# Latent attention in a two-block transformer kernel: queries and keys without position made channels first

## The chip, the cores and the metric

The kernel is one program on 1 core of one Trainium2 chip. The metric is device time in microseconds (us) of one launch, lower is better. Before the change it was timed in three runs: 1926.68 us in the median, from 1926.54 to 1927.67. TensorE does the matrix products, VectorE and ScalarE the elementwise work, GpSimd a few small steps, and SyncE issues the weight loads. The engines run their own instruction streams in order and wait for each other with semaphores.

## The reference

The first block runs twice (two layers), the second once. The change touches the latent attention (MLA) of the first block:

```python
def first_block(x, norm_g, w_in, diff_lambda, ..., mla_q_norm_g, w_uq, mla_kv_norm_g, w_ukv, w_out, final_norm_g):
    for l in range(DEPTH):                                   # DEPTH = 2, seq = 256, D_MODEL = 2048
        h = _rms_norm(x, norm_g[l])
        proj = jnp.einsum('bsd,de->bse', h, w_in[l])
        q_a, k_a, v_a, z_a, c_q, c_kv, k_r, z_b = jnp.split(proj, split_points, axis=-1)
        o_a = _diff_attention(qa, ka, va, lam, rel_bias_table)        # 8 heads, two softmaxes each
        o_a = _rms_norm(o_a, diff_subln_g[l]) * (1.0 - lambda_init)
        o_a = o_a.reshape(b, seq, DIFF_WIDTH) * jax.nn.silu(z_a)

        q_b = jnp.einsum('bsr,re->bse', _rms_norm(c_q, mla_q_norm_g[l]), w_uq[l])      # 512 -> 8 x (128 + 64)
        q_b = q_b.reshape(b, seq, MLA_HEADS, MLA_NOPE_DIM + MLA_ROPE_DIM)
        q_nope, q_rope = q_b[..., :MLA_NOPE_DIM], q_b[..., MLA_NOPE_DIM:]
        q_rope = _apply_rope(q_rope, cos[:, None, :], sin[:, None, :])
        kv = jnp.einsum('bsr,re->bse', _rms_norm(c_kv, mla_kv_norm_g[l]), w_ukv[l])    # 512 -> 8 x (128 + 128)
        kv = kv.reshape(b, seq, MLA_HEADS, MLA_NOPE_DIM + MLA_V_DIM)
        k_nope, v_b = kv[..., :MLA_NOPE_DIM], kv[..., MLA_NOPE_DIM:]
        k_rope = _apply_rope(k_r, cos, sin)
        o_b = _mla_attention(q_nope, q_rope, k_nope, k_rope, v_b)     # softmax((qn.kn + qr.kr) * scale, causal) v
        o_b = o_b.reshape(b, seq, MLA_WIDTH) * jax.nn.silu(z_b)

        x = x + jnp.einsum('bse,ed->bsd', jnp.concatenate([o_a, o_b], axis=-1), w_out[l])
    return _rms_norm(x, final_norm_g)
```

The second block (convolution, pooling, cross attention, a gated feed-forward) is not touched.

## The kernel before

**Products in three passes.** All inputs are 32-bit floats. A weight is loaded in units of 128 x 1024 numbers (512 KB) into one of four slots of `stage`. ScalarE rounds a unit to `w_hi` (L395), VectorE makes the rest `w_lo = stage - w_hi` (L400, `rest_unit`), and TensorE multiplies hi by hi, hi by lo and lo by hi into PSUM. Activations are kept channels first, split the same way (`xT`, `mT`). The slot of a unit is free once TensorE has used it (`unit_used`), so ScalarE and VectorE prepare unit u+3 (`LEAD`) while TensorE multiplies unit u.

**Two shapes of a unit.** `product_rows` (L437 to L439) holds the activations in the array and streams 512 weight columns: 12 matmuls of 512 columns in a unit, and the result has tokens on the partitions. `product_cols` (L453, L460) holds the weights and streams the tokens, hi and lo side by side: 8 matmuls of 512 columns (weight hi by both halves) and 8 of 256 (weight lo by hi); the result has channels on the partitions, in two halves that are added afterwards. The first block uses rows nearly everywhere, the feed-forward uses columns.

**PSUM.** `acc` is two pairs of banks, used in turn by the chunks of a stage. A product that starts a chunk waits until the pair has been read out (`banks_free`, counted by `acc_free0` and `acc_free1`). `aux` holds one bank for transposes (`tb`), two for scores, one for weights and outputs of heads.

**The stages of a layer.** After the first 56 units of w_in come the latent stage (32 units, here u = 0 to 31), the gate stage (32 units of w_in for the gates) and w_out (32 units). In the latent stage, units 0 to 15 make c_q and c_kv (512 columns each), 16 and 17 the rope key, 18 to 23 w_uq (three chunks of 512 columns, two units each), 24 to 31 w_ukv (four chunks). Heads of the differential attention are strewn in between, one in four units: after unit 4h the weights of head h-1 are transposed (L1117) and queries and keys of head h (L517), after unit 4h+1 come the outputs of head h-1 (L1123 to L1125) and the scores of head h (L1136). VectorE then makes the maxima (`diff_max`, L1995 to L2002) and two units later the weights (`diff_weights`, L2008 to L2014). The latents are turned to channels first after units 10, 11, 18 and 19 (`C_TURN`: transposes by TensorE, scale L528, round L535, rest L540). Their inverse roots `rstd_c` are made by `rsqrt` (L559 to L564, eleven small steps that wait for each other) at u = 19, after ScalarE's squares (L1707, at u = 16); ScalarE multiplies them in when it copies the w_uq and w_ukv chunks out of PSUM (L1720).

**The MLA heads** stand in the gate stage, one in four units. After unit 4h+2 `turn` (L517) transposes two blocks of queries (`qb`) and two of keys (`kvb`) of head h without position, ScalarE copies them to `qkT` (L1592), and after the next unit `mla_scores` (L1153, L1154) multiplies them. GpSimd applies the rope to `qb` and `kz` during the latent stage (L1002 to L1021).

The order of the work on each engine is written out by hand, by unit numbers.

## Time and profile before

| | us |
|---|---|
| median of three runs | 1926.68 |
| the profiled execution's own time | 1927.88 |
| its span, first to last instruction | 1926.1 |
| TensorE busy | 1914.7 (99%) |
| VectorE busy | 1433.1 (74%) |
| ScalarE busy | 1081.9 (56%) |
| GpSimd busy | 46.2 (2%) |
| mean granted TensorE clock | 0.998 of full speed |

The latent stage of layer 0 lies at about 179 to 286 us of the span, that of layer 1 at about 621 to 728; the gate stages follow. Busy time of an engine says how much it did, not whether anyone waited for it. For TensorE the starts of consecutive matmuls tell what one costs: a matmul's duration in the profile (0.39 us) is longer than the distance to the next one (0.23 us), since they overlap.

### The profile page before, as it was taken

The page shows a single profiled execution, that of the slowest core. Times are in us where ns is not written, and L with a number is a line of the kernel's source. Part 1 is how long each engine was busy: PE and PEld are TensorE (multiplying, and loading weights), DVE is VectorE, ACT ScalarE, POOL GpSimd, SP SyncE. Part 2 cuts the span into 40 slices and gives each one's busy share as a digit, 9 for nine tenths or more (in the row PEclk, how much of TensorE's full clock was granted, in tenths as well). Part 3 has the DMA queues.
Part 4 walks back from the last instruction along what each step waited for, and adds up shares of the span by engine and source line. Part 5 has one row for each costly group of instructions (what it writes and reads, how often), then busy time and mean ns, then how long its engine had stood idle before and what let it go on. Part 6 is the DMA issues. An engine that isn't in the chain of part 4 may idle for free.

```text
span 1926.1 us, 26620 instructions
## 1 busy us (share of the span) xinstructions
PE 1914.7 (99%) x9721; PEld 1623.2 (84%) x9721; DVE 1433.1 (74%) x2059; ACT 1081.9 (56%) x1598; POOL 46.2 (2%) x74
## 2 busy tenths in 40 slices
PE   9999999999999999999999999999999999999997
PEld 7888888888888888888888888888888888888886
DVE  7777675556877675655767766888878878899898
ACT  6555676655545676654644444655555555555554
POOL 1000030000000030000100000000000000000000
PEclk9999999999999999999999999999999999999999
DMA  9964445565665455555666455665666666666654
GB/s 347 309 210 133 143 154 158 151 206 185 209 209 167 139 162 176 142 164 186 212 187 194 154 166 184 186 185 182 199 188 191 188 185 191 190 219 197 204 192 161
DMA packets 248059, 361.29 MB, mean 188 GB/s; under 512 B 15505, under 2 KB 134497, under 8 KB 247457
## 3 DMA queue, kind: packets, MB, share of 16 engines
q1 hardware_dynamic: 246112, 353.15, 58.5%
q0 software_dynamic: 1568, 6.60, 1.0%
q8 instruction: 57, 0.93, 0.2%
q10 hardware_dynamic: 288, 0.33, 0.0%
q14 instruction: 34, 0.27, 0.0%
HBM read 356.88 MB, written 3.16 MB: 187 GB/s over the span
## 4 chain that ended last, share of the span: by engine, by line
PE 98%; DVE 1%; DMA 0%; ACT 0%; issue 0%; SPq 0%; DVEq 0%; ACTq 0%
PE acc L460 22%; PE acc L453 12%; PE acc L437 11%; PE acc L439 11%; PE acc L438 11%; PE acc L1206 4%; PE acc L1207 4%; PE acc L1205 4%; PE acc L1468 3%; PE acc L1469 3%; PE acc L1467 3%; PE aux L517 2%; PE aux L1468 1%; PE aux L1467 1%; PE aux L1469 1%; PE aux L1136 1%
## 5 line engine op out<-in xcount | busy, mean ns | idle before, releaser
L400 DVE TENSOR_TENSOR sb_w_lo<-sb_stage,sb_w_hi 128x1024 fp32r<-128x1024 f32 x476 | 583.0, 1227 | 272.2 <-ACT sb_w_hi L395 265.7
L395 ACT ACTIVATE sb_w_hi<-sb_stage 128x1024 fp32r<-128x1024 f32 x476 | 502.2, 1057 | 348.8 <-PE acc L453 122.7
L460 PE MATMUL acc<-sb_xT,sb_w_hi 128*128 128x512 f32 x1856 | 445.7, 391 | 0.0
L460 PEld LDWEIGHTS acc<-sb_xT,sb_w_hi 128*128 128x128 f32 x1856 | 340.8, 188 | 65.8
L453 PEld LDWEIGHTS acc<-sb_xT,sb_w_lo 128*128 128x128 f32 x1856 | 238.7, 191 | 9.3
L453 PE MATMUL acc<-sb_xT,sb_w_lo 128*128 128x256 f32 x1856 | 243.0, 283 | 0.0
L437 PE MATMUL acc<-sb_w_hi,sb_mT 128*128 128x512 f32 x544 | 217.3, 399 | 0.0
L439 PE MATMUL acc<-sb_w_hi,sb_mT 128*128 128x512 f32 x544 | 212.2, 390 | 0.0
L438 PE MATMUL acc<-sb_w_lo,sb_mT 128*128 128x512 f32 x544 | 212.1, 390 | 0.0
L437 PE MATMUL acc<-sb_w_hi,sb_xT 128*128 128x512 f32 x384 | 155.9, 406 | 0.0
L439 PE MATMUL acc<-sb_w_hi,sb_xT 128*128 128x512 f32 x384 | 150.0, 391 | 0.0
L438 PE MATMUL acc<-sb_w_lo,sb_xT 128*128 128x512 f32 x384 | 149.9, 390 | 0.0
L437 PEld LDWEIGHTS acc<-sb_w_hi,sb_mT 128*128 128x128 f32 x544 | 102.2, 188 | 22.7 <-issue 1.0
L439 PEld LDWEIGHTS acc<-sb_w_hi,sb_mT 128*128 128x128 f32 x544 | 102.1, 188 | 22.0
L438 PEld LDWEIGHTS acc<-sb_w_lo,sb_mT 128*128 128x128 f32 x544 | 102.3, 188 | 19.7
L1205 PE MATMUL acc<-sb_w_hi,sb_xT 128*128 128x512 f32 x220 | 85.7, 389 | 0.0
L1207 PE MATMUL acc<-sb_w_hi,sb_xT 128*128 128x512 f32 x220 | 85.6, 389 | 0.0
L1206 PE MATMUL acc<-sb_w_lo,sb_xT 128*128 128x512 f32 x220 | 85.6, 389 | 0.0
L439 PEld LDWEIGHTS acc<-sb_w_hi,sb_xT 128*128 128x128 f32 x384 | 72.1, 188 | 15.7
L437 PEld LDWEIGHTS acc<-sb_w_hi,sb_xT 128*128 128x128 f32 x384 | 72.2, 188 | 13.9
L740 ACT ACTIVATE sb_w_hi<-sb_pair_stage 128x1024 fp32r<-128x1024 f32 (+1 forms) x50 | 48.2, 982 | 62.2 <-DVE sb_pair_stage L753 53.5
L438 PEld LDWEIGHTS acc<-sb_w_lo,sb_xT 128*128 128x128 f32 x384 | 72.3, 188 | 12.7
(437 smaller groups left out, 2871.1 us busy)
## 6 DMA issues: line engine op xcount, KB each, us to landing
sb_stage<-w_in SPq DMA_DIRECT2D x232, 512.0 KB, 4.3
sb_stage<-w_up SPq DMA_DIRECT2D x176, 512.0 KB, 3.7
sb_stage<-w_out SPq DMA_DIRECT2D x96, 512.0 KB, 4.3
sb_stage<-w_down SPq DMA_DIRECT2D x54, 512.0 KB, 6.7
...
```

The source lines that it names most:

```text
L395: act.activation(w_hi[:, j % RING, 0:size], stage[:, j % RING, 0:size], ACT.Copy).then_inc(hi_ready, 1)
L400: dve.tensor_tensor(w_lo[:, j % RING, 0:size], stage[:, j % RING, 0:size], w_hi[:, j % RING, 0:size].bitcast(F32), ALU.subtract).then_inc( ...
L437: pe.matmul(o, x_hi, hi[:, k, :], start=first and k == 0, stop=False)
L438: pe.matmul(o, x_hi, lo[:, k, :], start=False, stop=False)
L439: mm = pe.matmul(o, x_lo, hi[:, k, :], start=False, stop=last and k == nk - 1)
L453: mm = pe.matmul(acc[:, 2 * pair + c, 0:SEQ], lo[:, k, c * P:(c + 1) * P], xT[:, k0 + k, 0, :], start=False, stop=False)
L460: mm = pe.matmul(acc[:, 2 * pair + c, :], hi[:, k, c * P:(c + 1) * P], both, start=first and k == 0, stop=last and k == 3)
L1205: pe.matmul(o, a(0), hi, start=start, stop=False)
L1206: pe.matmul(o, a(0), lo, start=False, stop=False)
L1207: return pe.matmul(o, a(1), hi, start=False, stop=stop)
L1467: pe.matmul(o, a(0), hi, start=start, stop=False)
L1468: pe.matmul(o, a(0), lo, start=False, stop=False)
```

## The change

- The weights w_uq and w_ukv are reordered on the host: all parts without position first, then the rope parts of w_uq and the values of w_ukv.
- In the latent stage, units 18 to 21 now make the queries without position, 24 to 27 the keys, in the shape by columns: four channel tiles of weights in a unit for 256 output channels (two heads), so each of these units is a chunk of its own. `product_latent_cols` issues 8 matmuls of 512 columns, then 8 of 256. Units 22 and 23 (rope parts, one chunk) and 28 to 31 (values, two chunks) stay by rows.
- Such a chunk is read out in two steps: ScalarE copies the right half to `cols_half` (`copy_cols`), VectorE adds the left half to it (`add_cols`) and frees the pair. Both stand one unit later in their streams, ahead of the preparation of a weight unit. The rows chunks are copied by ScalarE without a factor (`copy_rows`).
- Queries and keys are then channels first already: the eight transposes-of-four of the MLA heads in each layer and ScalarE's eight copies go.
- Roots: ScalarE scales c_kv itself before its turn (two instructions at u = 18), and VectorE applies the queries' root when it scales the scores (`query_scale`); `rsqrt` of the latents stands at u = 16 instead of 19. The turns of c_kv stand after units 19 and 21 instead of 18 and 19. `diff_max(4)` stands at u = 17 ahead of the rest of a unit, where it stood behind it.
- The mask is two blocks wide, and VectorE makes the scaled scores of a head in two steps of 256 and 128 columns where it took steps of 128 and 256.

```diff
-DIFF_TB = [2, 3, 4, 7, 8, 11, 12, 13]
-C_TURN = {10: (0, 0, 5), 11: (0, 1, 6), 18: (1, 0, 9), 19: (1, 1, 10)}
+DIFF_TB = [2, 3, 4, 7, 8, 10, 12, 13]
+C_TURN = {10: (0, 0, 5), 11: (0, 1, 6), 19: (1, 0, 9), 21: (1, 1, 11)}
...
+QUERY_COLS, KEY_COLS = {18 + n: n for n in range(4)}, {24 + n: n for n in range(4)}
+C_QUERY, C_ROPE, C_KEY, C_VALUE, C_Z, C_OUT = 9, 13, 14, 18, 20, 24
...
+        def product_latent_cols(pe, base, j, k0, pair):
+
+
+            pe.wait_ge(lo_ready, base + (j + 1))
+            hi, lo = (w[:, j % RING, :].rearrange("p (k n) -> p k n", n=256) for w in (w_hi, w_lo))
+            tiles = [(k, c) for k in range(4) for c in range(2)]
+            for k, c in tiles:
+                pe.matmul(acc[:, 2 * pair + c, :], hi[:, k, c * P:(c + 1) * P],
+                          mT[:, k0 + k, :, :].rearrange("p h t -> p (h t)"), start=k == 0, stop=False)
+            for k, c in tiles:
+                mm = pe.matmul(acc[:, 2 * pair + c, 0:SEQ], lo[:, k, c * P:(c + 1) * P], mT[:, k0 + k, 0, :],
+                               start=False, stop=k == 3)
+            mm.then_inc(unit_used, 1)
...
+        query_pair = lambda n: qb[:, n % 2, n // 2 * 512:(n // 2 + 1) * 512].rearrange("p (h t) -> p h t", h=2)
+        key_pair = lambda n: kvb[:, 0, n * 512:(n + 1) * 512].rearrange("p (h t) -> p h t", h=2)
+        query_of, key_of = (lambda h: query_pair(h // 2)[:, h % 2, :]), (lambda h: key_pair(h // 2)[:, h % 2, :])
+        value_of = lambda h, t: kvb[:, 1, t * WIDTH + h * DV:t * WIDTH + (h + 1) * DV]
+        output_of = lambda h, t: kvb[:, 0, h * SEQ + t * DV:h * SEQ + (t + 1) * DV]
+        rope_rows = lambda t: qb[:, t, WIDTH:WIDTH + HEADS * ROPE]
...
-                            pe.matmul(o, qkT[:, q * P:(q + 1) * P], qkT[:, 2 * P:2 * P + keys], start=True, stop=False)
+                            pe.matmul(o, query_of(h)[:, q * P:(q + 1) * P], key_of(h)[:, 0:keys], start=True, stop=False)
...
+                            if u in QUERY_COLS:
+                                c, i = C_QUERY - 6 + QUERY_COLS[u], 0
+                            if u in KEY_COLS:
+                                c, i = C_KEY - 6 + KEY_COLS[u], 0
+                            if u >= 28:
+                                c, i = C_VALUE - 6 + (u - 28) // 2, u % 2
...
+                        elif u in QUERY_COLS or u in KEY_COLS:
+                            product_latent_cols(pe, base, U_QKV + u, 0 if u < 24 else 4, c % 2)
...
+                            if j == 1:
+                                pe.wait_ge(ckv_scaled, layer + 1)
...
+                    def copy_cols(u, chunk):
+
+                        multiplied(act, quads * 4, U_QKV + u)
+                        if chunk not in (C_QUERY, C_KEY):
+                            evacuated(act, pairs, chunk - 1)
+                        pair = chunk % 2
+                        act.activation(cols_half[:, :, :], acc[:, 2 * pair:2 * pair + 2, SEQ:2 * SEQ], ACT.Copy)\
+                           .then_inc(cols_copied, 1)
+
+                    def copy_rows(u, chunk, dst):
+
+                        multiplied(act, quads * 4, U_QKV + u)
+                        for t in range(T):
+                            ins = act.activation(dst(t), acc[:, 2 * (chunk % 2) + t, :], ACT.Copy)
+                        ins.then_inc(acc_free[chunk % 2], 1)
+
+                    value_rows = lambda c: lambda t: kvb[:, 1, t * WIDTH + c * 512:t * WIDTH + (c + 1) * 512]
+
                     for u in range(32):
+                        if u - 1 in QUERY_COLS:
+                            copy_cols(u - 1, C_QUERY + QUERY_COLS[u - 1])
+                        if u - 1 in KEY_COLS:
+                            copy_cols(u - 1, C_KEY + KEY_COLS[u - 1])
+                        if u == 24:
+                            copy_rows(23, C_ROPE, rope_rows)
+                        if u == 30:
+                            copy_rows(29, C_VALUE, value_rows(0))
                         rounded(U_QKV + u)
+                        if u == 18:
+                            act.wait_ge(c_rstd, layer + 1)
+                            for t in range(T):
+                                ckv = qb[:, t, RANK:2 * RANK]
+                                ins = act.activation(ckv, ckv, ACT.Copy, scale=rstd_c[:, T + t:T + t + 1])
+                            ins.then_inc(ckv_scaled, 1)
...
-                        if u == 20 or (u > 20 and u % 2 == 1):
-                            c = (u - 19) // 2
-                            act.wait_ge(c_rstd, layer + 1)
-                            multiplied(act, quads * 4, U_QKV + 19 + 2 * c)
-                            for t in range(T):
-                                r = (0 if c < 3 else T) + t
-                                dst = qb[:, t, c * 512:(c + 1) * 512] if c < 3 else \
-                                    kvb[:, t, (c - 3) * 512:(c - 2) * 512]
-                                ins = act.activation(dst, acc[:, 2 * ((9 + c) % 2) + t, :], ACT.Copy,
-                                                     scale=rstd_c[:, r:r + 1])
-                            ins.then_inc(acc_free[(9 + c) % 2], 1)
                     for u in range(32):
+                        if u == 0:
+                            copy_rows(31, C_VALUE + 1, value_rows(1))
...
+                    def add_cols(chunk, dst):
+
+                        dve.wait_ge(cols_copied, layer * 8 + (chunk - C_QUERY if chunk < C_ROPE else chunk - C_KEY + 4) + 1)
+                        pair = chunk % 2
+                        dve.tensor_tensor(dst, acc[:, 2 * pair:2 * pair + 2, 0:SEQ], cols_half[:, :, :], ALU.add)\
+                           .then_inc(acc_free[pair], 1)
+
                     add_rows_qkv(5)
                     dve.wait_ge(bias_back, 16)
                     for u in range(32):
-                        if u == 18:
+                        if u - 1 in QUERY_COLS:
+                            add_cols(C_QUERY + QUERY_COLS[u - 1], query_pair(QUERY_COLS[u - 1]))
+                        if u - 1 in KEY_COLS:
+                            add_cols(C_KEY + KEY_COLS[u - 1], key_pair(KEY_COLS[u - 1]))
+                        if u == 16:
+                            step(dve.tensor_tensor(key_fold, ident[:, 0:ROPE], ident[:, ROPE:P], ALU.add))
+                            dve.wait_ge(c_squared, layer * 4 + 4)
+                            rsqrt(step, dve, rstd_c[:, :], sumsq_c[:, :], 4, RANK, done=c_rstd)
+                        if u == 17:
                             multiplied(dve, base, U_QKV + 17)
                             step(dve.tensor_copy(key_sum, acc[:, 0, SEQ:2 * SEQ]))
                             dve.tensor_tensor(key_sum, acc[:, 0, 0:SEQ], key_sum, ALU.add).then_inc(acc_free[0], 1)
-                        if u == 16:
-                            step(dve.tensor_tensor(key_fold, ident[:, 0:ROPE], ident[:, ROPE:P], ALU.add))
+                            diff_max(4)
                         if u % 4 == 3:
                             diff_weights(u // 4)
-                        if u == 19:
+                        if u in (19, 21):
                             j, t, use = C_TURN[u]
                             turn_scale(dve, tb0 + use, gain0 + (2 + 2 * j + t), gain_c[:, 4 * j:4 * j + 4])
                         rest(U_QKV + u)
@@ -2131,14 +2194,14 @@
                             evacuate_scaled(dve, base, U_QKV + u, j, 512, lambda t: qb[:, t, j * RANK:(j + 1) * RANK], rstd)
                         if u in C_TURN:
                             j, t, use = C_TURN[u]
-                            if u != 19:
+                            if j == 0:
                                 turn_scale(dve, tb0 + use, gain0 + (2 + 2 * j + t), gain_c[:, 4 * j:4 * j + 4])
                             turn_rest(dve, turn0 + (2 + 2 * j + t), token_part(mT, j, t, 0), token_part(mT, j, t, 1))
-                        if u % 4 == 1:
+                        if u == 20:
+                            dve.wait_ge(c_rstd, layer + 1)
+                            step(dve.tensor_scalar(query_scale[:, :], rstd_c[:, 0:T], MLA_SCALE, None, ALU.mult))
+                        if u % 4 == 1 and u != 17:
                             diff_max(u // 4)
-                        if u == 19:
-                            dve.wait_ge(c_squared, layer * 4 + 4)
-                            rsqrt(step, dve, rstd_c[:, :], sumsq_c[:, :], 4, RANK, done=c_rstd)
```

How the streams move, at three places. First VectorE in the latent stage of layer 0, from the fold of the rope key on; the names are `acc` (PSUM pair of a chunk), `sb_w_lo` (rest of a weight unit), `sb_turn_f` and `sb_mT` (turn of a latent), `sb_newton_v` (the root). Before:

```order
L2120 TENSOR_TENSOR sb_qb<-acc,sb_qb 128x256
L400 TENSOR_TENSOR sb_w_lo<-sb_stage,sb_w_hi 128x1024
L528 TENSOR_TENSOR sb_turn_f<-aux,sb_gain_c 128x512
L540 TENSOR_TENSOR sb_mT<-sb_turn_f,sb_mT 128x4x128
L2008 RECIPROCAL sb_inv_sum<-sb_row_sum 128x4
L2010 SCALAR_TENSOR_TENSOR sb_mix_f<-sb_row_sum,sb_lam_l,sb_inv_sum 128x2
L2012 SCALAR_TENSOR_TENSOR sb_s<-sb_s,sb_mix_f 128x256
L2014 SCALAR_TENSOR_TENSOR sb_s<-sb_s,sb_mix_f 128x128
L528 TENSOR_TENSOR sb_turn_f<-aux,sb_gain_c 128x512
L400 TENSOR_TENSOR sb_w_lo<-sb_stage,sb_w_hi 128x1024
L540 TENSOR_TENSOR sb_mT<-sb_turn_f,sb_mT 128x4x128
L559 TENSOR_SCALAR sb_newton_v<-sb_sumsq_c 128x4
```

And after the change, from the last step of the root to the first sum of halves:

```order
L580 SCALAR_TENSOR_TENSOR sb_rstd_c<-sb_newton_t,sb_rstd_c 128x4
L402 TENSOR_TENSOR sb_w_lo<-sb_stage,sb_w_hi 128x1024
L2183 COPY sb_qb<-acc 128x256
L2184 TENSOR_TENSOR sb_qb<-acc,sb_qb 128x256
L2043 SCALAR_TENSOR_TENSOR sb_s<-aux,sb_bias 128x512
L2045 SCALAR_TENSOR_TENSOR sb_s<-aux,sb_bias 128x256
L2048 TENSOR_REDUCE sb_neg_max<-sb_s 128x2
L2049 TENSOR_REDUCE sb_neg_max<-sb_s 128x2
L2050 TENSOR_SCALAR sb_neg_max<-sb_neg_max 128x4
L402 TENSOR_TENSOR sb_w_lo<-sb_stage,sb_w_hi 128x1024 x2
L2167 TENSOR_TENSOR sb_qb<-acc,sb_cols_half 128x512
```

The root has moved from behind the turns to ahead of the rest of unit 19; the fold of the rope key (L2183, L2184), the maxima of head 4 (L2043 to L2050) and two rests stand between it and the first sum of halves (L2167), which frees a pair.

Second, VectorE between the first two sums of halves, after the change:

```order
L2167 TENSOR_TENSOR sb_qb<-acc,sb_cols_half 128x512
L2056 RECIPROCAL sb_inv_sum<-sb_row_sum 128x4
L2058 SCALAR_TENSOR_TENSOR sb_mix_f<-sb_row_sum,sb_lam_l,sb_inv_sum 128x2
L2060 SCALAR_TENSOR_TENSOR sb_s<-sb_s,sb_mix_f 128x256
L2062 SCALAR_TENSOR_TENSOR sb_s<-sb_s,sb_mix_f 128x128
L544 TENSOR_TENSOR sb_turn_f<-aux,sb_gain_c 128x512
L402 TENSOR_TENSOR sb_w_lo<-sb_stage,sb_w_hi 128x1024
L556 TENSOR_TENSOR sb_mT<-sb_turn_f,sb_mT 128x4x128
```

The weights of head 4, a turn's two steps and a rest stand in front of the sum of unit 19's halves, which is the next row.

Third, TensorE around units 19 to 21 of the latent stage. Before, the end of unit 18, the turn behind it and the begin of unit 19:

```order
L439 MATMUL acc<-sb_w_hi,sb_mT 128x512
L517 MATMUL aux<-sb_ident,sb_qb 128x128 x4
L437 MATMUL acc<-sb_w_hi,sb_mT 128x512
L438 MATMUL acc<-sb_w_lo,sb_mT 128x512
L439 MATMUL acc<-sb_w_hi,sb_mT 128x512
```

After, the turn behind unit 19, unit 20, and the transposes behind it:

```order
L533 MATMUL aux<-sb_ident,sb_qb 128x128 x4
L481 MATMUL acc<-sb_mT,sb_w_hi 128x512 x8
L484 MATMUL acc<-sb_mT,sb_w_lo 128x256 x8
L1142 MATMUL aux<-sb_ident,sb_s 128x128 x3
L533 MATMUL aux<-sb_ident,sb_qa 128x128 x2
L533 MATMUL aux<-sb_ident,sb_kz 128x128 x2
```

Unit 20 (L481, L484) begins a chunk on the pair that unit 18 used; before, units 20 and 21 shared a chunk on the other pair than 18 and 19.

## Rows read from the trace of the kernel before

**Rows 1.** Page, part 1: busy us (share of the span) xinstructions.

```profile
PE 1914.7 (99%) x9721; PEld 1623.2 (84%) x9721; DVE 1433.1 (74%) x2059; ACT 1081.9 (56%) x1598; POOL 46.2 (2%) x74
```

**Rows 2.** Waits of TensorE: line, who released it, us in total, times, longest.

```profile
PE acc L1526 <- DVE sb_w_lo L747: 0.9, 1, 0.9
```

**Rows 3.** Timeline, TensorE, gate stage: start us, us, engine line operation.

```profile
296.57 0.38 PE L517 MATMUL aux<-sb_ident,sb_qb 128*128 128x128 f32 x2
...
296.92 0.48 PE L437 MATMUL acc<-sb_w_hi,sb_xT 128*128 128x512 f32 x1
297.24 0.40 PE L438 MATMUL acc<-sb_w_lo,sb_xT 128*128 128x512 f32 x1
...
309.59 0.38 PE L517 MATMUL aux<-sb_ident,sb_qb 128*128 128x128 f32 x2
...
309.95 0.47 PE L437 MATMUL acc<-sb_w_hi,sb_xT 128*128 128x512 f32 x1
```

**Rows 4.** The chain that ended last, in the second block: start us, us.

```profile
944.07 3.65 PE acc L460 x16
947.73 1.91 PE acc L453 x16
```

**Rows 5.** Timeline, TensorE: an undisturbed unit by rows and what follows it.

```profile
286.23 0.39 PE L437 MATMUL acc<-sb_w_hi,sb_xT 128*128 128x512 f32 x1
...
288.95 0.49 PE L1117 MATMUL aux<-sb_ident,sb_s 128*128 128x128 f32 x3
```

**Rows 6.** Timeline, TensorE: starts of unit 18 and the turn behind it, layer 0.

```profile
238.98 0.50 PE L437 MATMUL acc<-sb_w_hi,sb_mT 128*128 128x512 f32 x1
...
241.83 0.60 PE L517 MATMUL aux<-sb_ident,sb_qb 128*128 128x128 f32 x4
```

**Rows 7.** Timeline, ScalarE: end of the last square of the latents, layer 0.

```profile
237.49 0.19 ACT L1707 ACTIVATION_READ_ACCUMULATOR sb_junk<-sb_qb 128x1 f32 x1
```

**Rows 8.** Timeline, VectorE, latent stage of layer 0.

```profile
239.94 0.68 DVE L1995 SCALAR_TENSOR_TENSOR sb_s<-aux,sb_bias 128x512 f32<-128x512 f32 x1
...
242.12 0.42 DVE L2119 COPY sb_qb<-acc 128x256 f32<-128x256 f32 x1
...
242.91 1.22 DVE L400 TENSOR_TENSOR sb_w_lo<-sb_stage,sb_w_hi 128x1024 fp32r<-128x1024 f32 x1
...
246.03 0.17 DVE L2008 RECIPROCAL sb_inv_sum<-sb_row_sum 128x4 f32<-128x4 f32 x1
...
247.16 0.68 DVE L528 TENSOR_TENSOR sb_turn_f<-aux,sb_gain_c 128x512 f32<-128x512 f32 x1
247.75 1.22 DVE L400 TENSOR_TENSOR sb_w_lo<-sb_stage,sb_w_hi 128x1024 fp32r<-128x1024 f32 x1
248.89 0.69 DVE L540 TENSOR_TENSOR sb_mT<-sb_turn_f,sb_mT 128x512 fp32r<-128x512 f32 x1
249.49 0.17 DVE L559 TENSOR_SCALAR sb_newton_v<-sb_sumsq_c 128x4 f32<-128x4 f32 x1
...
251.54 1.22 DVE L400 TENSOR_TENSOR sb_w_lo<-sb_stage,sb_w_hi 128x1024 fp32r<-128x1024 f32 x1
```

**Rows 9.** Timeline, last products: VectorE's rest, and TensorE's start behind it.

```profile
1908.69 1.22 DVE L747 TENSOR_TENSOR sb_w_lo<-sb_stage,sb_w_hi 128x1024 fp32r<-128x1024 f32 x1
...
1909.97 0.50 PE L1526 MATMUL acc<-sb_w_hi,sb_act_T 128*128 128x512 f32 x1 [0.95 <-DVE sb_w_lo L747]
```

**Rows 10.** Timeline, TensorE: first matmul behind the scores of head 7.

```profile
280.66 0.50 PE L437 MATMUL acc<-sb_w_hi,sb_mT 128*128 128x512 f32 x1
```

**Rows 11.** Timeline, VectorE: maxima of that head, idle before them in brackets.

```profile
280.78 0.69 DVE L1995 SCALAR_TENSOR_TENSOR sb_s<-aux,sb_bias 128x512 f32<-128x512 f32 x1 [1.49 <-PE aux L1136]
```

**Rows 12.** Timeline, VectorE: two rests beside GpSimd's rope, then maxima.

```profile
262.71 3.48 DVE L400 TENSOR_TENSOR sb_w_lo<-sb_stage,sb_w_hi 128x1024 fp32r<-128x1024 f32 x2 [0.42 <-ACT sb_w_hi L395]
267.35 0.69 DVE L1995 SCALAR_TENSOR_TENSOR sb_s<-aux,sb_bias 128x512 f32<-128x512 f32 x1 [1.16 <-PE aux L1136]
```

**Rows 13.** Timeline, GpSimd: a step of the rope of the queries.

```profile
263.51 1.60 POOL L1018 TENSOR_TENSOR sb_kz<-sb_qb,sb_rope 128x256 f32<-128x256 f32 x1
```

120 lines of the change are left out of this document (59 added, 61 removed).

## The prediction

> **What bounds the kernel now.** I read part 1 of the page first: TensorE is busy 99% of the span, VectorE 74% [rows 1]. The waits of TensorE come next. Behind the first microseconds they name one that counts, 0.9 us in the last products [rows 2]; in both latent stages and both gate stages it waits for nobody. So TensorE's stream is the critical path, and the change is worth what it takes out of that stream, less what it puts in, less every wait that it creates there: nothing downstream gives a wait back. The third view is the timeline, for two questions: what an instruction costs on TensorE (the distance between starts, not the duration shown), and at what time VectorE gets to each step of the latent stage of layer 0. Layer 1 runs the same streams, so each result counts twice.
>
> **What goes.** Eight turns of the MLA heads in each layer, four transposes each. Alone, a turn starts at 296.57, the next product at 296.92, and the matmul behind that 0.32 us later instead of 0.23: 0.35 + 0.09 = 0.44 us. Seven of the eight stand right behind the transposes of another head's weights, where the slow first matmul is paid anyway: 309.59 to 309.95, 0.36 us [rows 3]. A layer: 0.44 + 7 x 0.36 = 2.96; both: **-5.9 us**. ScalarE's copies to qkT go with them; ScalarE is 56% busy and nobody on the path waits for it there, so they are worth nothing directly.
>
> **What TensorE gets.** Sixteen units change shape, eight in a layer. By columns, 16 long matmuls start within 3.65 us and 16 short ones within 1.91 [rows 4], so a unit is half of the sum, 2.78 us. By rows an undisturbed unit takes 286.23 to 288.95, 2.72 us [rows 5]. 0.06 x 16 = **+1.0 us**. The scores read queries and keys from other tiles in the same shape: 0, since the matmul is the same.
>
> **What waits.** A chunk was two units; a chunk by columns is one. TensorE begins unit 20 on the pair that unit 18 filled, 2.8 us after unit 18's end plus a turn, and in that time ScalarE must copy one half and VectorE must add the other. The question is when VectorE gets there. I follow its new order with the old durations.
>
> The root now stands ahead of the rest for unit 19 and waits for ScalarE's squares, which end at 237.68 [rows 7]. From there: the root, 249.49 to 251.54, 2.05 us; a rest, 247.75 to 248.89, 1.14; fold of the rope key, 242.12 to 242.91, 0.79; maxima of head 4, 239.94 to 242.12, 2.18; two more rests, 2.28 [rows 8]. That is 246.12. The sum of halves reads 512 columns from PSUM and from SBUF. No row shows it; the nearest is the first step of the maxima, 0.68 with the same kinds of input [rows 8]; from below the two small steps of the fold bound it at 0.4, from above a rest at 1.22. I take 0.68: 246.80, and 0.06 until TensorE starts, as at 1909.91 to 1909.97 [rows 9]: 246.86. TensorE gets there at 238.98 + 2.85 (unit 18 starts and ends as before [rows 6]) + 0.06 (its new shape) + 2.78 (unit 19) + 0.36 (the turn behind it) = 245.03. **Wait at unit 20: 1.83 us.** The copy on ScalarE is not the last to come, since ScalarE can take it as soon as unit 18 ends at 241.9. The rest for unit 20 itself is ready at 245.0, a tie.
>
> Unit 21 needs the pair of unit 19. VectorE, from 246.12: the sum 0.60 in its stream, weights of head 4 1.13 (246.03 to 247.16), scale 0.59, rest 1.14, rest of the turn 0.60 (248.89 to 249.49), sum 0.68 [rows 8]: 250.86, with the start 250.92. TensorE: 246.86 + 2.78 + 0.09 + seven transposes of 0.09 = 250.36. **Wait: 0.56 us.**
>
> Units 22 to 26 I find covered: behind unit 21 TensorE has the fold of the key, outputs, scores and a turn, over 2 us, and unit 22 and 23 are one chunk. Unit 27 waits for the sum of unit 25's halves, and that stands behind the maxima of head 6, whose scores TensorE issues only behind unit 25. VectorE begins such maxima 0.12 us after the next product begins [rows 10, 11]; 0.12 + 2.18 + 0.68 + 0.06 = 3.04 against 2.87 for unit 26. **Wait: 0.17 us,** and a first matmul of 0.50 instead of 0.39 behind a wait [rows 9], 0.28 together. At units 20 and 21 that slow first matmul is already paid for the transposes ahead of them.
>
> While TensorE waits, its queue holds the products of the unit and the heads' steps behind it; ScalarE and VectorE lose nothing, they are ahead. A layer: 1.83 + 0.56 + 0.28 = 2.67; both: **+5.3 us**.
>
> **GpSimd's neighbourhood.** Its rope of the queries overlaps the rests for units 27 and 28: the two took 3.48 us, where two rests alone take 2.4, beside a step of GpSimd's that took 1.60 [rows 12, 13]. Maxima in the same stretch kept their 0.69 [rows 12]. By my reading, steps with two SBUF inputs collide, steps that read PSUM do not. Before, the lead of three units covered it. Now, between units 24 and 28, each pair waits for a sum behind a rest, so up to the 1.1 us lost there could appear at unit 27 or 28: from 0 to 1.1 in a layer. The layer's rope starts at about the same unit, but falls on other steps; I take 0.25 in a layer, nearer to nothing, since only one rest stands between the scores of head 6 and the sum that matters: **+0.5 us**. The Trainium skill (GPSIMD Engine Reference, Specifications) says that GpSimd shares its SBUF interfaces with VectorE and contends with instructions that have two SBUF inputs; the trace agrees, with 3.48 for two rests and 0.69 for the maxima. By it, the new sums themselves, which have one SBUF input, would stay at 0.68 beside the rope, and only rests and weights would stretch.
>
> **Edits at nothing.** The two scalings of c_kv by ScalarE are new, and the turn behind unit 19 waits for them. They can begin when the root is there, at 239.7, and are due when unit 19 ends, at 244.7: 5 us for 1024 columns, which VectorE takes 1.22 for in a rest [rows 8]. With that cover gone they would cost what they are late. Maxima of MLA heads: 256 and 128 columns instead of 128 and 256, the same. Loads: the same number and size at the same places of SyncE's queue, in rows half as long; three units of lead cover them. GpSimd waits for one chunk instead of two and must be done eight units later.
>
> **The sum.** -5.9 + 1.0 + 5.3 + 0.5 = **+0.9 us**. The profiled execution took 1927.88, so 1928.8 by its own time; it stands 1.2 above the median of the runs, 1926.68, and against that median I predict **1927.6 us**. A measurement of this kernel can tell about 0.2%, 3.9 us, from no change.
>
> **The rivals.**
> - *Exchange of transposes for waits*, as above. For it: the chain to unit 20 has no slack left in it and is made of measured steps. Against: it assumes that no step of VectorE starts earlier than in my order. Its own range, with 0.3 us of error on each of three waits and 0 to 1.1 for the collision: 1925.5 to 1930.5. Chance 0.66.
> - *The waits are hidden*: the pairs come free in time, because TensorE reaches unit 20 later than I think or the squares end earlier. For it: before, TensorE never waited here, and VectorE has a quarter of its time free [rows 1]. Against: it would need 1.8 us, all of it at one place. -5.9 + 1.0 = -4.9: 1921.8. Chance 0.11.
> - *Slower, by GpSimd's collision at unit 27*: the rope of the queries falls on the rests of units 28 and 29, and the sums of units 25 and 26 slip by 1.1 us each, one after the other, with no lead to take it. It decides if a collision stands between the scores of head 6 and unit 28. 2.2 us a layer in place of 0.25: +0.9 + 3.9 = +4.8, 1931.5. For it: 3.48 for two rests [rows 12]. Against: GpSimd's steps that collide are few. Chance 0.16.
> - *The change doesn't do what it says*: the root comes one unit sooner, but nothing that waits for it was late, and being sooner is what puts 2.05 us and a wait for the squares ahead of three rests. If the rests for units 19 and 20 come late as well by about 0.5 us each, that is +2 over the sum: 1929.6. Chance 0.07.
>
> **How the numbers follow.** Faster by over 0.2%: only the second case, 0.11. Slower: the third, and a tail of the first and last, 0.17. Within: 0.72. The range is to leave out 2 in 10: it reaches from 1923.5, between the first and the second case, to 1931.5, the price of the third.
>
> **What would show it.** Right: MATMULs of `turn` on `sb_kvb` in the gate stage halved, and those on `sb_qb` down to the latents' own; waits of TensorE in the latent stage released by VectorE's L2167, two of 1.8 and two of 0.6 us, at about 245 and 250 of the span and 442 us later; the gate stage shorter by 3 us, the latent stage longer by about 3. Wrong: no wait at L481 (then 1921.8), or waits over 1 us at units 26 to 28 with long L402 beside GpSimd (then 1931).

## The result, and the profile of the changed kernel

| | before | changed |
|---|---|---|
| median of 13 runs each, us | 1927.27 | 1931.46 |
| their range | 1926.54 to 1928.48 | 1929.73 to 1933.09 |
| ratio, 95% interval | | 1.0021 [1.0014, 1.0028] |
| span of the profiled execution | 1926.1 | 1930.0 |
| its own time | 1927.88 | 1931.84 |

The change made the kernel 4.2 us slower, 0.21%, and the interval of the ratio does not reach down to 1. I had forecast 0.9 us more, 1927.6, with a range to 1931.5. The number lies inside the range, but at its very end, and the loss is over four times the forecast one: that it is inside is luck.

The page of the changed kernel, part 1 and the first line of part 4, against [rows 1]:

```profile
PE 1912.6 (99%) x9721; PEld 1621.2 (84%) x9721; DVE 1443.8 (75%) x2077; ACT 1073.2 (56%) x1586; POOL 48.7 (3%) x74
...
PE 94%; DVE 4%; DMA 1%; ACT 1%; issue 0%; SPq 0%; DVEq 0%; ACTq 0%
```

TensorE's busy time fell by 2.1 us, and the span still grew by 3.9: TensorE stands still for 6 us that it did not stand still before. In the chain, VectorE's share went up from 1% to 4%. The waits of TensorE say where (line <- who released it: us in total, times, longest), against [rows 2]:

```profile
PE acc L481 <- DVE sb_qb L2167: 4.0, 4, 1.8
PE acc L481 <- DVE sb_kvb L2167: 1.6, 2, 0.8
PE acc L1555 <- DVE sb_w_lo L771: 1.4, 1, 1.4
```

L481 is the first matmul of a unit by columns, L2167 VectorE's sum of halves, which frees the pair. Four waits are at units 20 and 21, two at unit 27. The timeline of TensorE in layer 0, at these places (start, us, and the idle time before in brackets):

```profile
239.50 2.14 PE L481 MATMUL acc<-sb_mT,sb_w_hi 128*128 128x512 f32 x8
...
242.44 2.12 PE L481 MATMUL acc<-sb_mT,sb_w_hi 128*128 128x512 f32 x8
...
245.35 0.60 PE L533 MATMUL aux<-sb_ident,sb_qb 128*128 128x128 f32 x4
247.72 2.11 PE L481 MATMUL acc<-sb_mT,sb_w_hi 128*128 128x512 f32 x8 [1.77 <-DVE sb_qb L2167]
...
251.78 0.50 PE L481 MATMUL acc<-sb_mT,sb_w_hi 128*128 128x512 f32 x1 [0.24 <-DVE sb_qb L2167]
...
274.89 0.50 PE L481 MATMUL acc<-sb_mT,sb_w_hi 128*128 128x512 f32 x1 [0.80 <-DVE sb_kvb L2167]
```

The idle time in brackets is not the whole loss. Without a wait, the next matmul starts 0.16 to 0.25 us ahead of the shown end of the one before. Counted from that follow-on, unit 20 loses 2.02 us, unit 21 0.49, unit 27 0.96, and unit 24, which the view of waits does not list at all, 0.24.

To say where time went I cut each layer at three starts on TensorE that both kernels have: the first product of the rope key (L477, now L493), the transposes of the rope key in the first gate unit (`ident,sb_kz`), and the first product of the output weights on `mT` (L437, now L439). Below, "latent stage" means the first stretch: the second half of the latent stage, from u = 16 on, and the first gate unit. The rest of the gate stage is the second stretch. Here are the three starts of layer 0 before the change, then of the changed kernel:

```profile
232.93 0.39 PE L477 MATMUL acc<-sb_xT,sb_w_hi 128*128 128x512 f32 x1
...
289.27 0.38 PE L517 MATMUL aux<-sb_ident,sb_kz 128*128 128x128 f32 x2
...
399.61 0.48 PE L437 MATMUL acc<-sb_w_hi,sb_mT 128*128 128x512 f32 x1
```

```profile
233.46 0.39 PE L493 MATMUL acc<-sb_xT,sb_w_hi 128*128 128x512 f32 x1
...
294.33 0.27 PE L533 MATMUL aux<-sb_ident,sb_kz 128*128 128x128 f32 x1
...
401.43 0.48 PE L439 MATMUL acc<-sb_w_hi,sb_mT 128*128 128x512 f32 x1
```

| us | before | changed | difference |
|---|---|---|---|
| latent stage, layer 0 (layer 1) | 56.34 (56.35) | 60.87 (60.87) | +4.53 (+4.52) |
| gate stage | 110.34 (110.34) | 107.10 (107.10) | -3.24 (-3.24) |
| both stages, both layers | | | +2.57 |
| from the first gate stage's end to layer 1's start | | | +0.27 |
| ahead of layer 0's latent stage | | | +0.53 |
| from layer 1's gate stage to the last wait | | | +0.02 |
| the last wait (L1555) and behind it | | | +0.5 |

The stages repeat to 0.05 us from layer to layer and, below, between kernels that do the same there; the two ends of the program do not. The product that stands at 9.51 us before and at 9.84 after starts anywhere from 8.67 to 9.84 in all the profiles, and the last wait takes from nothing to 1.6.

Of the 0.53 us ahead of layer 0's latent stage, 0.33 are there at that product. The other 0.2 grow bit by bit between 196 and 233 us, in units 0 to 15, and 0.2 of the 0.27 between the layers grow in the same units of layer 1. That part repeats: from about 16 us to the rope key it is 217.4 us before and 217.6 in eight of the ten kernels below that keep the change. What makes it, no run shows. So 3.0 us of the change's loss are located; the other 0.9 of this pair of profiles lie where single executions differ. The measured ratio allows 2.7 to 5.4 us.

The gate stage is where the turns were. Before, weights and a turn behind them took 0.68 us, from this start to the product at 309.95 [rows 3]; now it is 0.25 (before, then the changed kernel):

```profile
309.27 0.38 PE L1117 MATMUL aux<-sb_ident,sb_s 128*128 128x128 f32 x2
```

```profile
313.83 0.49 PE L1142 MATMUL aux<-sb_ident,sb_s 128*128 128x128 f32 x3
314.08 0.48 PE L439 MATMUL acc<-sb_w_hi,sb_xT 128*128 128x512 f32 x1
```

### The profile page after: what moved, and what is told of

It reads as the page before. It is cut to its first block, busy times and chain, and to the rows that moved or that the text cites. A ratio compares the mean times of both kernels' runs of the same rounds, so it can differ in the third digit from the quotient of the medians.

```text
span 1930.0 us, 26624 instructions
## 1 busy us (share of the span) xinstructions
PE 1912.6 (99%) x9721; PEld 1621.2 (84%) x9721; DVE 1443.8 (75%) x2077; ACT 1073.2 (56%) x1586; POOL 48.7 (3%) x74
## 4 chain that ended last, share of the span: by engine, by line
PE 94%; DVE 4%; DMA 1%; ACT 1%; issue 0%; SPq 0%; DVEq 0%; ACTq 0%
PE acc L462 22%; PE acc L455 11%; PE acc L439 10%; PE acc L440 10%; PE acc L441 10%; PE acc L1225 4%; PE acc L1227 4%; PE acc L1226 4%; PE acc L1496 2%; PE acc L1497 2%; PE acc L1498 2%; PE aux L533 1%; PE acc L481 1%; PE aux L1496 1%; PE aux L1497 1%; PE aux L1161 1%
## 5 line engine op out<-in xcount | busy, mean ns | idle before, releaser
L439 PE MATMUL acc<-sb_w_hi,sb_mT 128*128 128x512 f32 x480 | 191.4, 399 | 0.0
L440 PE MATMUL acc<-sb_w_lo,sb_mT 128*128 128x512 f32 x480 | 187.3, 390 | 0.0
L441 PE MATMUL acc<-sb_w_hi,sb_mT 128*128 128x512 f32 x480 | 187.2, 390 | 0.0
L439 PE MATMUL acc<-sb_w_hi,sb_xT 128*128 128x512 f32 x384 | 156.4, 407 | 0.0
L439 PEld LDWEIGHTS acc<-sb_w_hi,sb_mT 128*128 128x128 f32 x480 | 90.2, 188 | 19.8 <-issue 1.0
L441 PEld LDWEIGHTS acc<-sb_w_hi,sb_mT 128*128 128x128 f32 x480 | 90.2, 188 | 19.5
L440 PEld LDWEIGHTS acc<-sb_w_lo,sb_mT 128*128 128x128 f32 x480 | 90.3, 188 | 17.5
L439 PEld LDWEIGHTS acc<-sb_w_hi,sb_xT 128*128 128x128 f32 x384 | 72.2, 188 | 14.2
```

The source lines that it names most:

```text
L439: pe.matmul(o, x_hi, hi[:, k, :], start=first and k == 0, stop=False)
L440: pe.matmul(o, x_hi, lo[:, k, :], start=False, stop=False)
L441: mm = pe.matmul(o, x_lo, hi[:, k, :], start=False, stop=last and k == nk - 1)
```

## Who holds unit 20

VectorE and then ScalarE of the changed kernel, layer 0, ahead of unit 20:

```profile
238.31 0.17 DVE L575 TENSOR_SCALAR sb_newton_v<-sb_sumsq_c 128x4 f32<-128x4 f32 x1 [2.33 <-ACT sb_junk L1764]
...
240.38 1.22 DVE L402 TENSOR_TENSOR sb_w_lo<-sb_stage,sb_w_hi 128x1024 fp32r<-128x1024 f32 x1
...
244.40 0.17 DVE L2050 TENSOR_SCALAR sb_neg_max<-sb_neg_max 128x4 f32<-128x4 f32 x1
244.48 2.35 DVE L402 TENSOR_TENSOR sb_w_lo<-sb_stage,sb_w_hi 128x1024 fp32r<-128x1024 f32 x2
246.98 0.69 DVE L2167 TENSOR_TENSOR sb_qb<-acc,sb_cols_half 128x512 f32<-128x512 f32 x1
```

```profile
244.60 0.51 ACT L1627 ACTIVATE sb_s<-sb_s,sb_neg_max 128x256 f32<-128x256 f32 x1 [1.65 <-DVE sb_neg_max L2050]
...
246.38 0.57 ACT L1721 ACTIVATE sb_cols_half<-acc 128x512 f32<-128x512 f32 x1
```

The sum (L2167) takes 0.69 us, as forecast. It starts at 246.98 because two things end there nearly together: two rests on VectorE, at 246.83, and ScalarE's copy of the other half, at 246.95. Unit 18 was done at 242.4, but the copy stands in ScalarE's queue behind the exponentials of head 4, which wait for VectorE's maxima. The prediction followed VectorE alone and said that the copy was "not the last to come". The copy is the last to come, by a little: VectorE starts a step up to 0.1 us ahead of the shown end of the one before (the rests at 244.48, with the negation shown to 244.57), so behind the rests alone the sum could have started at about 246.75. It starts 0.23 later, 0.03 behind the copy's end.

## The experiments

All ran in five rounds beside the kernel before on the same chip (the changed kernel's row is that of the result): 5 runs of e2, 6 of e7, 10 or 11 of each of the others. The ratios are to the kernel before, whose median was 1926.96 to 1927.06 in these rounds; the last two columns are the two stretches of layer 0.

| kernel | median us | ratio, 95% interval | latent | gate |
|---|---|---|---|---|
| changed | 1931.46 | 1.0021 [1.0014, 1.0028] | 60.87 | 107.10 |
| e1 copies | 1930.10 | 1.0016 [1.0007, 1.0025] | 60.61 | 107.10 |
| e2 sums | 1934.35 | 1.0042 [1.0029, 1.0056] | 63.13 | 107.10 |
| e3 both | 1927.36 | 1.0002 [0.9993, 1.0011] | 59.27 | 107.10 |
| e4 root | 1928.01 | 1.0005 [0.9996, 1.0014] | 59.65 | 107.09 |
| e5 ordered | 1924.83 | 0.9988 [0.9979, 0.9997] | 58.04 | 107.10 |
| e6 GpSimd short | 1929.78 | 1.0014 [1.0005, 1.0023] | 60.05 | 107.10 |
| e7 no turns (of before) | 1920.94 | 0.9966 [0.9954, 0.9979] | 56.37 | 107.03 |
| e8 root alone (of before) | 1931.63 | 1.0025 [1.0015, 1.0034] | 58.42 | 110.36 |
| e9 last | 1922.67 | 0.9979 [0.9970, 0.9988] | 57.23 | 107.10 |
| e10 no negation | 1928.30 | 1.0005 [0.9996, 1.0014] | 59.81 | 107.10 |
| e11 all | 1923.29 | 0.9980 [0.9971, 0.9989] | 57.17 | 107.10 |

**e1 to e3: the two causes, one at a time and together.**

```diff
 # e1, ScalarE (e3 has it too)
+                        if u == 18:
+                            copy_cols(18, C_QUERY)
                         if r == 2:
                             exps(h, ...)
+                        if u in (19,):
+                            copy_cols(u, C_QUERY + QUERY_COLS[u])
 # e2, VectorE (e3 has it too, and unit 19's sum behind diff_weights(4))
                             diff_max(4)
+                            add_cols(C_QUERY, query_pair(0))
 # each taken out of its old place, at the head of the next unit
```

> Changed kernel, with ScalarE's copies of the first halves of units 18 and 19 one place earlier in its own queue (unit 18 ahead of the exponentials of head 4, unit 19 right behind unit 19's place and ahead of the round of the turned block); VectorE's order as it is. Theory A (unit 20 waits for a sum of halves that stands in VectorE's queue behind two rests of 2.35 us that end at 246.9 us, and behind a copy that ends at 246.95: two causes that end together, so taking away the copy's alone gives nothing): +4.2 us against the kernel before, as the changed kernel, +-0.7. Rival C (ScalarE's late copy alone holds the sum): unit 20 starts 2.0 us and unit 21 0.5 us sooner in each layer, -0.8 us against the kernel before. Rival B (units by columns are slow in themselves, or GpSimd): +4.2.

> Changed kernel, with VectorE's sum of halves of unit 18 right behind the maxima of head 4, ahead of the two rests; ScalarE's order as it is. Theory A: VectorE now stands at the sum until the copy ends at 246.95, so unit 20 gains nothing, and the rests of units 17 and 18, and all behind them, come 2.4 us later: the lo parts of the next weights are late and TensorE waits for them, about 2 us more in each layer, +8 us against the kernel before. If VectorE's rests alone were the cause: unit 20's 2.0 us go, 0 us. Rival B: +4.2 us, the idle time only moves.

> Changed kernel with both: ScalarE's copies of units 18 and 19 earlier, and VectorE's sums of them earlier (unit 18 behind the maxima of head 4, unit 19 behind head 4's weights). Theory A: the waits of unit 20 (2.02 us beyond an undisturbed follow-on) and of unit 21 (0.49) go in each layer, up to 0.7 us of it comes back since rests stand 0.7 us later: -3.6 us to -5.0 us against the changed kernel, +0.6 us against the kernel before. Rival B: +4.2 us.

With the copies early, the latent stage is 0.26 us shorter, 60.61 for 60.87, and the kernel 3.1 us slower than before, where +4.2 +-0.7 was expected. That 0.26 is the little by which the copy came last; the sum now follows VectorE's rests at once, and all the others of unit 20's 2 us stay (VectorE of e1):

```profile
246.56 0.68 DVE L2172 TENSOR_TENSOR sb_qb<-acc,sb_cols_half 128x512 f32<-128x512 f32 x1
```

With the sums early alone VectorE stands at the sum, and everything behind it is late (VectorE of e2, then the first of its waits of TensorE; it is VectorE's rest for unit 20 that is missing now):

```profile
245.97 0.69 DVE L2168 TENSOR_TENSOR sb_qb<-acc,sb_cols_half 128x512 f32<-128x512 f32 x1 [2.41 <-ACT sb_cols_half L1722]
246.58 2.35 DVE L403 TENSOR_TENSOR sb_w_lo<-sb_stage,sb_w_hi 128x1024 fp32r<-128x1024 f32 x2
```

```profile
PE acc L482 <- DVE sb_w_lo L403: 6.0, 2, 3.0
```

Behind that wait the two layers differ. Here are the stretches of unit 20 in layer 0 and layer 1 of e2 (stretch, its length, busy time of PE, PEld, DVE, ACT and POOL, granted clock, DMA share, GB/s):

```profile
247.90:252.30 4.40, 4.36 (x16) 3.67 (x17) 4.33 (x8) 1.61 (x3) 0.00 (x0) 0.63 0.69 209
693.40:696.30 2.90, 2.88 (x17) 2.58 (x18) 2.83 (x7) 0.13 (x1) 0.00 (x0) 1.00 0.57 183
```

In layer 0 TensorE had been idle for 3.02 us, and the granted clock is 0.63 in the mean: the first products start 0.43 us apart instead of 0.23, which is the lower level (1.2 instead of 2.4 GHz) for most of the unit. In layer 1, behind 3.00 us, it is 1.00. It costs nothing here: from unit 20's start to unit 21's it is 5.11 us in both layers, since at full clock TensorE only waits 1.33 us longer for the sum of unit 19. In the other kernels the waits of the latent stages are 1.9 us or less, and both layers take the same.

With both, the sum comes at 243.70, ahead of the rests, and the waits on `sb_qb` are gone from the list. What is left are unit 27's and one of half a microsecond for weights, since the rests stand 0.7 us later. VectorE of e3, then its waits of TensorE:

```profile
243.70 0.68 DVE L2173 TENSOR_TENSOR sb_qb<-acc,sb_cols_half 128x512 f32<-128x512 f32 x1
244.30 2.35 DVE L404 TENSOR_TENSOR sb_w_lo<-sb_stage,sb_w_hi 128x1024 fp32r<-128x1024 f32 x2
```

```profile
PE acc L483 <- DVE sb_kvb L2173: 1.6, 2, 0.8
...
PE acc L483 <- DVE sb_w_lo L404: 1.0, 2, 0.5
```

The latent stage gives back 1.60 us in each layer, the median 4.1 in all. -0.3, +2.3 and -1.6 us a layer for the one, the other and both: theory A, with both causes real and each all but hidden behind the other. By the medians e3 is 0.4 us slower than the kernel before (+0.6 expected) and e2 7.4 (+8). Rival B, that the units themselves are slow, is out as the cause of these waits.

**e4 and e8: the root.**

```diff
 # e4, of the changed kernel (e8: the reverse, in the kernel before, from behind unit 19's steps)
                         if u == 16:
                             step(dve.tensor_tensor(key_fold, ...))
-                            dve.wait_ge(c_squared, layer * 4 + 4)
-                            rsqrt(step, dve, rstd_c[:, :], sumsq_c[:, :], 4, RANK, done=c_rstd)
                         ...
                         rest(U_QKV + u)
+                        if u == 16:
+                            dve.wait_ge(c_squared, layer * 4 + 4)
+                            rsqrt(...)
```

> Changed kernel with one thing moved: the latent's root stands behind the rest of unit 16 instead of ahead of it, so that the rest's 1.2 us lies in the 2.33 us that VectorE waits for the squares. Theory A (what counts is how late VectorE's queue is at the sum of unit 18, yet ScalarE's exponentials follow from VectorE's maxima, so copy and sum both come sooner by what the root gives back): unit 20 0.8 to 1.2 us sooner in each layer, +2.2 us against the kernel before. Rival B: +4.2 us.

> The kernel before with the latent's root alone moved to where the change has it, ahead of VectorE's rest of unit 16. If the root is free there (VectorE has slack in the latent stage, as the prediction took it): 0 us. If it is not (VectorE stands 2.3 us for the squares, and then the root's 2.15 us lie ahead of the rests, the scaling of the turned latent and the maxima of head 4): a turn or a unit waits about 2 us in each layer, +4 us.

One rest of 1.2 us moved into VectorE's 2.33 us of idle time ahead of the root shortens the stage by 1.22 us in each layer; the median is 1.0 us above the kernel before (+2.2 expected). And the kernel before with nothing but the root at its new place is 4.6 us slower, as much as the whole change. Its trace shows how; TensorE and VectorE of e8:

```profile
247.19 0.63 PE L517 MATMUL aux<-sb_ident,sb_qb 128*128 128x128 f32 x4 [1.87 <-DVE sb_turn_f L528]
```

```profile
237.93 0.17 DVE L559 TENSOR_SCALAR sb_newton_v<-sb_sumsq_c 128x4 f32<-128x4 f32 x1 [2.28 <-ACT sb_junk L1707]
...
240.00 2.35 DVE L400 TENSOR_TENSOR sb_w_lo<-sb_stage,sb_w_hi 128x1024 fp32r<-128x1024 f32 x2
...
246.36 0.68 DVE L528 TENSOR_TENSOR sb_turn_f<-aux,sb_gain_c 128x512 f32<-128x512 f32 x1
```

VectorE waits 2.28 us for the squares and then needs two more for the root; rests, maxima and the scaling of the turned latent slide by that, and the second turn of TensorE waits for the bank. VectorE has a quarter of the span free, but not here. The places of the losses differ: in e8 the turn waits, in the changed kernel, where that turn stands elsewhere, unit 20 does. So the two costs must not be added. How much of the changed kernel's waits a still later root would take away, no run tells, and the maxima of head 4, which the change moved ahead of a rest, were not tried alone.

**e7: what the turns are worth.** The turn and its copy were taken out of `z_heads` on TensorE and ScalarE, and the uses of the bank renumbered. The kernel leaves out work that its result needs.

> The kernel before without the 16 turns of queries and keys without position and without ScalarE's 16 copies of them (work left out: the scores of the latent heads read the last block of the first eight). It measures the term that the change wins: -5.9 us by the prediction's prices (0.44 alone, 0.36 behind the weights' turns), -6.4 by the shift of the gate stages in the changed kernel's trace (0.40 each); 0 if ScalarE or VectorE is what the gate stage follows.

6.1 us by the medians, and the gate stage 110.34 to 107.03, 3.31 a layer, 0.41 a turn. The gain was real and slightly larger than priced.

**e6 and e10: GpSimd.** First the rows. The changed kernel's VectorE behind the scores of head 6, then its GpSimd:

```profile
272.81 0.41 DVE L2049 TENSOR_REDUCE sb_neg_max<-sb_s 128x2 f32<-128x256 f32 x1
273.25 0.99 DVE L2050 TENSOR_SCALAR sb_neg_max<-sb_neg_max 128x4 f32<-128x4 f32 x1
274.16 0.68 DVE L2167 TENSOR_TENSOR sb_kvb<-acc,sb_cols_half 128x512 f32<-128x512 f32 x1
```

```profile
272.93 1.29 POOL L1040 TENSOR_TENSOR sb_kz<-sb_qb,sb_rope 128x512 f32<-128x512 f32 x1
```

The negation of four columns, 0.17 us elsewhere, takes 0.99. It ends at 274.24, GpSimd's instruction at 274.22. In e5 the same pair ends at 271.26 and 271.23.

```diff
 # e6: GpSimd's rope of the queries on a part of the heads, in all its five steps (work left out)
-                        step(pool.tensor_tensor(qr[...], halves, by_head(cos, HEADS, 2), ALU.mult))
+                        step(pool.tensor_tensor(qr[...][:, 0:1], halves[:, 0:1], by_head(cos, 1, 2), ALU.mult))
 # e10: VectorE
-                        step(dve.tensor_reduce(neg_max[:, 2:4], ..., AX_X, ALU.max))
-                        dve.tensor_scalar(neg_max[:, :], neg_max[:, :], -1.0, None, ALU.mult).then_inc(row_max, 1)
+                        dve.tensor_reduce(neg_max[:, 2:4], ..., AX_X, ALU.max, negate=True).then_inc(row_max, 1)
```

> Changed kernel in which GpSimd turns the positions of one head's queries instead of eight (work left out), so its instructions beside units 24 to 28 are short; nothing is moved. Theory G (the wait of unit 27 is GpSimd's: VectorE's small negation took 0.99 us instead of 0.17 beside GpSimd's 1.29 us): unit 27 waits 0.15 instead of 0.96 beyond a follow-on, -1.6 us against the changed kernel, +2.6 against the kernel before. Rival (unit 27 waits for the maxima's place in the queue alone): +4.2.

> Changed kernel in which the maxima of the first eight heads come out of VectorE's two reductions with their sign turned, so that the small negation of 4 columns behind them (0.17 us, but 0.99 us at head 6, where it ends within 0.02 us of GpSimd's instruction of 1.29 us) is gone; GpSimd works as in the changed kernel. Lock theory (the negation, one input and output in SBUF, stood until GpSimd's instruction was done; reductions and the sum, whose second input is PSUM, don't): unit 27's 0.96 us beyond a follow-on fall to about 0.1, and unit 20 comes 0.1 us sooner: latent stage 0.9 us shorter in each layer, -1.9 us against the changed kernel, +2.3 us against the kernel before. Rival (anything of VectorE's beside that instruction of GpSimd's is held up by it): the reduction or the sum takes the 0.8 us, and only 0.1 to 0.2 us a layer go: +3.9 us.

e6: the negation is back to 0.17 and unit 27's wait is gone; the stage loses 0.82 us. VectorE of e6:

```profile
271.96 0.17 DVE L2050 TENSOR_SCALAR sb_neg_max<-sb_neg_max 128x4 f32<-128x4 f32 x1
272.04 0.68 DVE L2167 TENSOR_TENSOR sb_kvb<-acc,sb_cols_half 128x512 f32<-128x512 f32 x1
```

e10 tells whether the negation alone is held or anything of VectorE's. GpSimd's instruction is as long as ever, and beside it VectorE's reduction and sum keep their times. VectorE, then GpSimd of e10:

```profile
272.76 0.42 DVE L2049 TENSOR_REDUCE sb_neg_max<-sb_s 128x2 f32<-128x256 f32 x1
273.10 0.68 DVE L2167 TENSOR_TENSOR sb_kvb<-acc,sb_cols_half 128x512 f32<-128x512 f32 x1
```

```profile
272.76 1.30 POOL L1040 TENSOR_TENSOR sb_kz<-sb_qb,sb_rope 128x512 f32<-128x512 f32 x1
```

GpSimd can be the one that is held, too. In the changed kernel the rest ahead of the maxima of head 6 starts 0.13 us before a step of GpSimd's. The rest keeps its time, and the step takes 1.68 us; in e5, with no rest beside it, the same step takes 0.74 (VectorE, then GpSimd):

```profile
269.40 1.22 DVE L402 TENSOR_TENSOR sb_w_lo<-sb_stage,sb_w_hi 128x1024 fp32r<-128x1024 f32 x1
```

```profile
269.53 1.68 POOL L1044 TENSOR_TENSOR sb_kz<-sb_kz 128x256 f32<-128x256 f32 x1
```

In e10 the stage is 1.06 us shorter, so 2.1 in both layers, with 1.9 expected. By the medians it is 3.2; the further 1.1 are not in the stages.

**e5, e9, e11: the exchange in a better order.** e5 has the edits of e3 and e4 and unit 25's copy and sum ahead of the maxima of head 6; e9 adds the same for unit 26; e11 adds e10's edit.

> Changed kernel with the orders of e3 and e4 together, and unit 25's copy and sum ahead of the maxima of head 6 as well. Theory A (the exchange is right, and the waits are a matter of the order in VectorE's and ScalarE's queues): all four waits of a layer (units 20, 21, 24, 27: 3.7 us beyond an undisturbed follow-on) go, and what stays is the turns taken out (6.4 us by the gate stages' shift) against 16 units that take 0.1 us more each: -4.8 us against the kernel before, about 1922.2. Rival (what is late moves on to the next thing, the rests or the turns): -1 to -2 us against the kernel before.

> e5's kernel with unit 26's copy ahead of the exponentials of head 6 and its sum ahead of the rest of unit 26, as unit 18's. In e5's trace unit 28 starts 0.69 us later than an undisturbed follow-on in each layer, since the sum of unit 26 waits for a copy that stands behind those exponentials, and these behind VectorE's negation (1.01 us beside GpSimd). Theory A: that wait goes, -1.4 us against e5, -3.6 us against the kernel before (1923.4). Rival (the exponentials or the rests, 0.6 us later each, become the wait): -2.2 us, as e5.

> e9's kernel with e10's edit. In e9's trace no wait of TensorE stands in the latent stage but 0.25 us at unit 24, behind VectorE's maxima of head 5 and the sum of unit 21. By theory A that wait alone can shrink, by 0.1 us a layer: -4.5 us against the kernel before, 0.2 us below e9, not to be told from it.

e5 came to 2.2 us under the kernel before, not 4.8: of the four waits three went, unit 24's 0.25 stayed, and a new one came up behind them. Its VectorE, ScalarE and TensorE show the same pattern one unit on, a copy behind exponentials behind the stretched negation:

```profile
270.25 1.01 DVE L2058 TENSOR_SCALAR sb_neg_max<-sb_neg_max 128x4 f32<-128x4 f32 x1
...
273.67 0.69 DVE L2175 TENSOR_TENSOR sb_kvb<-acc,sb_cols_half 128x512 f32<-128x512 f32 x1 [1.29 <-ACT sb_cols_half L1723]
```

```profile
273.06 0.58 ACT L1723 ACTIVATE sb_cols_half<-acc 128x512 f32<-128x512 f32 x1
```

```profile
274.41 0.50 PE L441 MATMUL acc<-sb_w_hi,sb_mT 128*128 128x512 f32 x1 [0.53 <-DVE sb_kvb L2175]
```

e9 takes that one away, and no wait of the latent stages is left in its list. It beats both kernels: 1922.67, 4.3 us or 0.21% under the kernel before (3.6 expected) and 8.8 under the changed one. e11 is not to be told from it, as expected (3.7 us under the kernel before, 4.5 expected): with nothing waiting behind the maxima, dropping the negation gains 0.06 us in the stage. e9's latent stage is still 0.89 us longer than before's. 0.25 is unit 24; the rest, 0.64, I put down to the units by columns.

## The prediction, step by step

| term, both layers, us | forecast | measured |
|---|---|---|
| 16 turns out | -5.9 | -6.5 (gate stages) |
| 16 units by columns | +1.0 | +1.6 (what the waits leave of +4.53 a layer) |
| wait at unit 20 | +3.7 | +4.0 |
| wait at unit 21 | +1.1 | +1.0 |
| unit 24 | 0 | +0.5 |
| unit 27, order and GpSimd | +1.1 | +1.9 |
| units 0 to 15, and between the layers | 0 | +0.5 |
| sum | +0.9 | +3.0 |

- **What bounds, and that a wait is not given back: right.** The gate stage is 107.09 or 107.10 in ten kernels whose latent stages range from 57.2 to 63.1 us.
- **The turns: right, 0.04 each too small.** The cost is what vanishes between the neighbours, 0.68 less 0.25; I had taken only the distance from the transposes' start to the next product.
- **Units 20 and 21: right in place and size, half right in cause.** VectorE's order with old durations gave 247.39 for unit 20 when shifted by this trace's later start; it was 247.72. But the step "the copy on ScalarE is not the last to come" failed. I had asked when the data were ready, not what stood in ScalarE's queue: exponentials that wait for maxima. It cost little in the sum, 0.2 to 0.3 us a layer (the 0.23 above, 0.26 by e1), since VectorE's rests end almost at the same time; but it would have led anyone astray who mended VectorE's order alone (e2, 7.4 us slower than the kernel before).
- **"Units 22 to 26 I find covered": wrong at unit 24,** which came 0.24 us late, since the sum of unit 21 stands behind the maxima of head 5.
- **GpSimd: the step that failed most.** I took 0.25 us a layer "since only one rest stands between the scores of head 6 and the sum that matters". That rest, at 269.40, kept its 1.22 us. What was hit is the negation, and at the worst place: 0.82 a layer by e6. It has both ends in SBUF and a single input; the reductions ahead of it have that too and were not held, so my sorting by inputs could not tell them apart. The maxima that I had read before [rows 12] fell on no such moment. The rule that I quoted, from the Trainium skill (GPSIMD Engine Reference, Specifications), names two kinds of VectorE instruction, those with two SBUF inputs and those in a 2-port performance mode, and I used the first only. The Trainium skill (SBUF — State Buffer, Who interferes with whom) counts `tensor_scalar` among those that can enter that mode, says that `tensor_reduce` on trn2 never contends, and that whoever issues first has the shared ports for the whole instruction while the other blocks. The traces agree in what they show: 0.99 us ending with GpSimd's instruction, which had started 0.3 us sooner; reduction 0.42 and sum 0.68 beside it; GpSimd's 1.68 behind a rest that had started first. That the negation ran in such a mode, no run shows.
- **Units by columns: 0.08 to 0.10 instead of 0.06 each.** Behind another unit one can take 2.79 us (242.00 to 244.79 in e5), but most stand behind a turn, weights or scores, and in the changed kernel all eight take 2.86 to 2.94, where units by rows in the same places take 2.82 to 2.86, and 2.72 behind another unit. I had priced all sixteen by a long row of units in the second block [rows 4]. Unit 19 stands right behind unit 18 and still takes 2.91 in the changed kernel. In all the kernels with the root ahead of the rest it is 2.89 to 2.91, with the root behind it (e4, e5, e9, e11) 2.80, so 0.1 of e4's 1.22 is there; why, the traces don't say.
- **The c_kv scalings at nothing: right.** ScalarE has done them at 242.96, and the turn behind unit 19 starts at 245.35 with no wait.
- **The rivals.** "Slower by GpSimd's collision" had the measured time, 1931.5, and the right place, between the scores of head 6 and unit 28, but not the measured reason: its rests were not what was held, and the collision was worth 1.6 us, not 4.4. "The waits are hidden" is out. "The change doesn't do what it says" had 7 in 100 and said that the root's place is what makes it late: e4 and e8 bear that out (-3.4 and +4.6 us by the medians, -2.4 and +4.2 by the stages); its own reason, that the rests for units 19 and 20 come late, is not in the changed kernel's waits. My sum did contain the root, as part of VectorE's order.
- **The signs.** The waits came where I said, released by L2167, and the gate stage got 3.2 us shorter. But the latent stage got 4.5 us longer, not about 3, and unit 24 came late as well.
- **The sum.** Of the 3.3 us between 0.9 and 4.2, 2.1 are the terms above, the largest of them unit 27, 0.8 more than forecast. The rest I can't place: it is within the interval, and the ends of the program vary by as much. The range was wide enough for a sum that had the sign and the main terms right and missed over three quarters of the loss.
